# A two-layer encoder trunk with a top-2 expert FFN on one core: the row-number matmuls move to an expert's third step, the first loads change order, and the tail of the attention goes by token tile

## The chip, the cores and the metric

The kernel runs on one core of one Trainium2 chip. It is written engine by engine: TensorE (PE), VectorE (DVE), ScalarE (ACT), GpSimd (POOL) and SyncE (SP) each have a program of their own, and semaphores order them. The metric is the device time of one execution in microseconds. Before the change it is 1575.75 us, the median of 3 runs (1575.65 to 1578.21).

## The reference, cut to what matters

Two layers over 256 tokens of width 1024, all in float32.

```python
for l in range(2):
    h = rms_norm(x, g_mix[l])
    qa, ka, va, qb, kb, vb, qc, kc, vc, qd, kd, vd, fd = split(h @ w_in[l])
    oa = stick_breaking_attention(qa, ka, va)
    ob = sliding_window_sink_attention(norm(qb), norm(kb), vb, sinks, slopes)
    oc = chunked_relpos_attention(norm(qc), norm(kc), vc, rel_bias[l])
    od = forgetting_attention(norm(qd), norm(kd), vd, log_sigmoid(fd + b_f[l]))
    x = x + concat(rms_norm(o) * g_out for o in (oa, ob, oc, od)) @ w_out[l]
    h2 = rms_norm(x, g_ffn[l])
    if l == 0:   # dense, hidden width 2816
        x = x + (silu(h2 @ w_gate) * (h2 @ w_up)) @ w_down
    else:        # 8 experts of hidden width 3584, the best two for each token
        gates = softmax of the two largest of h2 @ w_router, else 0
        x = x + sum(gates[:, e] * swiglu(h2, w_gate[e], w_up[e], w_down[e]) for e in range(8))
```

## The kernel before, in words

**Tokens and weights.** The 256 tokens are two tiles of 128. SBUF holds nine units of 4096 floats per partition, through which all weights pass; only SyncE's queue loads weights. The attention's matmuls are plain float32. In the FFN each weight and each activation is split into a rounded high part and a low remainder, and a product is three matmuls: high by high, high by low, low by high (lines 825 to 827 for dense gate and up, 939 to 941 for an expert's, 849 to 851 for down). The high part is made by ScalarE (`high`, line 1139), the low part by VectorE (`low`, line 1555), each in four quarters; a quarter of a full unit is 128x1024 elements.

**Attention.** The groups come in the order D, A, C, B. `project` (line 634) multiplies by the input weights. GpSimd makes the reciprocal roots (`rstd`, lines 1240 and 1243) and, once in each layer, group C's bias table (line 1284, 8 additions). That table comes from `ext`, a scratch tensor in DRAM with each row of the relative bias extended by copies of its last element; SyncE writes it with two DMAs (`extend`, lines 488 and 491), waits for them, and loads the table with overlapping rows (`load_table`, line 496). Everything that SyncE issues behind this wait starts after it. `out_project` (line 757) sums over the groups for token tile t; the order before is D, A for tile 0, C for tile 0, D and A for tile 1, then B's transposes (line 707) and values (lines 728 to 730), C for tile 1, B for tile 0, B for tile 1. Then VectorE adds the sum to x (line 1487), ScalarE squares (line 1010), GpSimd makes the root, VectorE scales (line 1319), TensorE transposes (`norm`, line 616), and ScalarE and VectorE read the transposes (lines 1020 and 1331, in layer 1 also 1340). This is done for both tiles before the dense steps or the router (line 883) begin.

**Dense FFN.** 2816 hidden columns are a half step of 256 and five steps of 512. `hidden_cols` puts the half step first. Each step does gate and up for tile 0, down of the step before for tile 1, the transposes of the hidden product (line 834), and so on for tile 1. The hidden product needs ScalarE's SiLU (line 1152) and VectorE's product (line 1561). `steps` writes the first steps out and puts the last four into a loop of two turns.

**Experts.** At most 128 tokens go to an expert, in slots. An expert has 7 steps of 512 hidden columns. In `slots_path` a step m is: gate (`half_up(m, 0)`), up (`half_up(m, 1)`), down of the step before (`slot_down(m - 1)`), transposes of this step's product. For the next expert VectorE makes a selection matrix (`select`, line 1650) at the end of an expert's step 0; TensorE multiplies it by the token numbers (`index`, line 908) between gate and up of step 1; VectorE reads the row numbers (line 1657); GpSimd gathers the rows from DRAM (line 1297), and TensorE transposes them at the end of step 4 (line 918). GpSimd also stores each expert's output rows (line 1301).

VectorE's order in a step is: low part of the next gate, hidden product, (row numbers in step 1), low part of the next up, low part of the hidden product, low part of down, (selection in step 0). ScalarE's is: SiLU, high part of the next gate, of the next up, of the hidden product, of down.

Of the kernel before, what the change touches and what calls it, by code (L numbers as in the profile page):

```python
# [15 lines left out]
P = 128  # L16
# [4 lines left out]
L = 2  # L21
# [116 lines left out]
def trunk(nc, x_in, g_mix, w_in, b_f, g_q, g_k, swa_sinks, rel_bias, g_out, w_out, g_ffn,  # L138
          w_ff_gate, w_ff_up, w_ff_down, w_router, w_exp_gate, w_exp_up, w_exp_down, consts, out):
    with ExitStack() as ctx:  # L140
# [95 lines left out]
        oT = xs  # L236

# [45 lines left out]
        lo_ready = [sem(f"low_{kind}_ready") for kind in ("gate", "up", "down")]  # L283
        s_ext = sem("rel_bias_extended")
        s_tabc = sem("rel_table_loaded")
# [91 lines left out]
        def steps(eng, one, n, first, use, parity):  # L377
# [3 lines left out]
            peeled = n - 4  # L381
            for s in range(peeled):
                one(s, (parity + s) % 2, first + s, use + (parity + s) // 2, None)
            with eng.Fori(0, 2) as i:
# [19 lines left out]
        def unless_last(eng, s, n, loop, run):  # L404

            if s < n - 3:
                run()
                return
# [13 lines left out]
        def hidden_cols(s, dense):  # L422
            return FT // 2 if dense and s == 0 else FT
# [31 lines left out]

        block = ctx.enter_context(nc.Block())
# [3 lines left out]
        def _(sp):  # L460
# [24 lines left out]
            def extend():  # L485

                rows = ext.rearrange("l h c -> (l h) c")
                sp.dma_start(rows[:, 0:RB - 1], rel_bias.rearrange("l h c -> (l h) c")[:, 1:RB]).then_inc(s_ext, 16)
                last = bass.AP(tensor=rel_bias.tensor, offset=rel_bias.offset + RB - 1, 
                               ap=[[RB, L * H], [0, EXT - RB + 1], [1, 1]])  # L490
                sp.dma_start(rows[:, RB - 1:EXT].unsqueeze(2), last).then_inc(s_ext, 16)

            def load_table(l):

                sp.wait_ge(s_ext, 16 * 2)
                sp.dma_start(hankels[l], bass.AP(tensor=ext.tensor, offset=ext.offset + l * H * EXT,
                                             ap=[[1, P], [EXT, H], [1, T]])).then_inc(s_tabc, 16)
# [11 lines left out]
            load_w_in_d(0)  # L509
            sp.dma_start(con[:, P:C_ALL], consts[:, P:C_ALL]).then_inc(s_con, 16)  # L510
# [6 lines left out]
            load_w_in(0, "A")  # L517
            extend()
            load_table(0)
# [6 lines left out]
            def first_steps(l, gate, up, down, cols):  # L526

                if l == 0:
# [13 lines left out]
                load_up(gate, l, 1, 0, cols)  # L542
                load_up(up, l, 1, 1, cols)
                if l == 0:
                    load_down(down, l, 1, cols)
# [12 lines left out]
            with sp.Fori(1, DENSE_STEPS // 2) as i:  # L558
# [1234 lines left out]
```

## Time and profile before

| | |
|---|---|
| median of 3 runs | 1575.75 us (1575.65 to 1578.21) |
| the profiled execution | 1572.12 us, span 1570.3 us |
| mean granted TensorE clock | 0.979 of full speed |
| busy: TensorE, VectorE, ScalarE, GpSimd | 95%, 70%, 58%, 4% |
| attention 0, dense steps, attention 1 | to about 182, 376 and 545 us |
| router and experts | from 545 us to the end |

The granted clock is TensorE's: 1.00 in a stretch is 2.4 GHz, 0.50 is 1.2 GHz. In a row of the timeline the first two numbers are the start and the duration in us, then come engine, line, operation, output and inputs, shapes and the count of instructions; what stands in brackets is how long the engine had been idle before the row, and who ended that.

### The profile page before, as it was taken

The page shows a single profiled execution, that of the slowest core. Times are in us where ns is not written, and L with a number is a line of the kernel's source. Part 1 is how long each engine was busy: PE and PEld are TensorE (multiplying, and loading weights), DVE is VectorE, ACT ScalarE, POOL GpSimd, SP SyncE. Part 2 cuts the span into 40 slices and gives each one's busy share as a digit, 9 for nine tenths or more (in the row PEclk, how much of TensorE's full clock was granted, in tenths as well). Part 3 has the DMA queues.
Part 4 walks back from the last instruction along what each step waited for, and adds up shares of the span by engine and source line. Part 5 has one row for each costly group of instructions (what it writes and reads, how often), then busy time and mean ns, then how long its engine had stood idle before and what let it go on. Part 6 is the DMA issues. An engine that isn't in the chain of part 4 may idle for free.

```text
span 1570.3 us, 16689 instructions
## 1 busy us (share of the span) xinstructions
PE 1486.3 (95%) x6513; PEld 1149.1 (73%) x6513; DVE 1092.0 (70%) x1248; ACT 907.7 (58%) x1206; POOL 61.7 (4%) x99
## 2 busy tenths in 40 slices
PE   6999799998999879999999999999999999999997
PEld 3565578886565457887887887887887887888885
DVE  1244464442233467888998888898898899798894
ACT  2133343342233256777777777777777777677772
POOL 1021000000021000000000000000000000000000
PEclk9999899999999989999999999999999999999999
DMA  7710464419030248999999999999999999999992
GB/s 237 284 55 0 176 253 161 161 60 402 7 129 33 103 165 334 353 372 376 374 360 374 370 359 371 377 365 366 375 356 364 384 367 368 355 359 363 393 343 82
DMA packets 181786, 435.20 MB, mean 277 GB/s; under 512 B 6545, under 2 KB 11849, under 8 KB 181577
## 3 DMA queue, kind: packets, MB, share of 16 engines
q1 hardware_dynamic: 178824, 423.63, 73.4%
q0 software_dynamic: 2880, 10.49, 1.7%
q8 instruction: 51, 0.84, 0.2%
q14 instruction: 31, 0.25, 0.1%
HBM read 428.34 MB, written 5.78 MB: 276 GB/s over the span
## 4 chain that ended last, share of the span: by engine, by line
PE 86%; DVE 7%; ACT 2%; DMA 2%; issue 2%; SPq 1%; POOL 0%; DVEq 0%; ACTq 0%
PE ps L939 12%; PE ps L941 12%; PE ps L940 12%; PE ps L849 8%; PE ps L851 8%; PE ps L850 8%; PE ps L634 7%; PE ps L757 3%; DVE unit_rounded L1555 3%; PE ps L826 3%; PE ps L827 3%; PE ps L825 3%; DMA wmem<-in_w_in_dram 2%; PE ps L834 2%; ACT unit_rounded L1139 1%
## 5 line engine op out<-in xcount | busy, mean ns | idle before, releaser
L1555 DVE TENSOR_TENSOR unit_rounded<-wmem,unit_rounded 128x1024 fp32r<-128x1024 f32 (+1 forms) x744 | 854.4, 1211 | 90.4 <-ACT unit_rounded L1139 90.3
L1139 ACT ACTIVATE unit_rounded<-wmem 128x1024 fp32r<-128x1024 f32 (+1 forms) x744 | 719.7, 1043 | 150.2 <-PE ps L941 82.1
L849 PE MATMUL ps<-unit_rounded,vbuf_rounded 128*128 128x512 f32 x536 | 212.6, 397 | 4.5 <-DVE unit_rounded L1555 3.0
L851 PE MATMUL ps<-unit_rounded,stage_rounded 128*128 128x512 f32 x536 | 212.7, 397 | 0.0
L850 PE MATMUL ps<-unit_rounded,vbuf_rounded 128*128 128x512 f32 x536 | 212.4, 396 | 0.0
L939 PE MATMUL ps<-unit_rounded,qkT_rounded 128*128 128x512 f32 x448 | 181.4, 405 | 2.4 <-DVE qkT_rounded L1698 2.4
L940 PE MATMUL ps<-unit_rounded,qkT_rounded 128*128 128x512 f32 x448 | 178.6, 399 | 0.0
L941 PE MATMUL ps<-unit_rounded,qkT_rounded 128*128 128x512 f32 x448 | 178.5, 398 | 0.0
L939 PE MATMUL ps<-unit_rounded,hT_rounded 128*128 128x512 f32 x448 | 177.2, 396 | 0.0
L941 PE MATMUL ps<-unit_rounded,hT_rounded 128*128 128x512 f32 x448 | 174.6, 390 | 0.0
L940 PE MATMUL ps<-unit_rounded,hT_rounded 128*128 128x512 f32 x448 | 174.5, 390 | 0.0
L634 PE MATMUL ps<-wmem,hT 128*128 128x512 f32 (+2 forms) x448 | 160.7, 516 | 6.3 <-DMA wmem<-in_w_in_dram 4.9
L634 PEld LDWEIGHTS ps<-wmem,hT 128*128 128x128 f32 x448 | 85.9, 195 | 74.4 <-issue 67.3
L849 PEld LDWEIGHTS ps<-unit_rounded,vbuf_rounded 128*128 128x128 f32 x536 | 101.1, 189 | 29.1 <-issue 3.2
L851 PEld LDWEIGHTS ps<-unit_rounded,stage_rounded 128*128 128x128 f32 x536 | 101.0, 188 | 24.4
L850 PEld LDWEIGHTS ps<-unit_rounded,vbuf_rounded 128*128 128x128 f32 x536 | 101.1, 189 | 24.2
L1156 ACT ACTIVATE vbuf_rounded<-ps 128x512 fp32r<-128x512 f32 (+1 forms) x68 | 40.1, 589 | 132.4 <-PE ps L834 132.4
L939 PEld LDWEIGHTS ps<-unit_rounded,qkT_rounded 128*128 128x128 f32 x448 | 85.3, 190 | 21.8 <-DVE qkT_rounded L1698 2.6
L941 PEld LDWEIGHTS ps<-unit_rounded,qkT_rounded 128*128 128x128 f32 x448 | 85.2, 190 | 20.7
L940 PEld LDWEIGHTS ps<-unit_rounded,qkT_rounded 128*128 128x128 f32 x448 | 85.2, 190 | 19.1
L941 PEld LDWEIGHTS ps<-unit_rounded,hT_rounded 128*128 128x128 f32 x448 | 84.1, 188 | 17.8
L940 PEld LDWEIGHTS ps<-unit_rounded,hT_rounded 128*128 128x128 f32 x448 | 84.2, 188 | 16.7
(207 smaller groups left out, 1319.9 us busy)
## 6 DMA issues: line engine op xcount, KB each, us to landing
wmem<-in_w_exp_gate_dram SPq DMA_DIRECT2D x56, 2048.0 KB, 8.7
wmem<-in_w_exp_up_dram SPq DMA_DIRECT2D x56, 2048.0 KB, 9.0
wmem<-in_w_exp_down_dram SPq DMA_DIRECT2D x56, 2048.0 KB, 9.1
wmem<-in_w_in_dram SPq DMA_DIRECT2D x4, 3072.0 KB, 16.1
wmem<-in_w_ff_gate_dram SPq DMA_DIRECT2D x5, 2048.0 KB, 8.4
wmem<-in_w_ff_up_dram SPq DMA_DIRECT2D x5, 2048.0 KB, 8.6
wmem<-in_w_ff_down_dram SPq DMA_DIRECT2D x5, 2048.0 KB, 7.6
wmem<-in_w_out_dram SPq DMA_DIRECT2D x4, 2048.0 KB, 19.0
```

Of the source, the lines that this page charges most:

```text
L634: mm = pe.matmul(pbank(m)[:, 0:cols], hT[:, k, t * P:(t + 1) * P], win(l, g)[:, k, c0:c0 + cols], start=(k == 0), stop=(k == KD - 1))
L757: mm = pe.matmul(ps[:, 2 * t + half, :], oT[:, t, k * P:(k + 1) * P], wo[:, k, half * 512:(half + 1) * 512], start=(g == ORDER[0] and kk = ...
L825: pe.matmul(o, xhk, hi[:, k, :], start=(k == 0), stop=False)
L826: pe.matmul(o, xhk, lo[:, k, :], start=False, stop=False)
L849: pe.matmul(o, hhb, hi[:, b, c], start=(first and b == 0), stop=False, skip_group_check=True)
L850: pe.matmul(o, hhb, lo[:, b, c], start=False, stop=False, skip_group_check=True)
L851: mm = pe.matmul(o, hlb, hi[:, b, c], start=False, stop=(b == blocks - 1), skip_group_check=True)
L939: pe.matmul(o, xhk, hi[:, k, :], start=(k == 0), stop=False)
L940: pe.matmul(o, xhk, lo[:, k, :], start=False, stop=False)
L941: mm = pe.matmul(o, xlk, hi[:, k, :], start=False, stop=(k == KD - 1))
L1139: act.activation(quarter_r(HIGH[l][kind], q, cols), quarter(SETS[l][i][kind], q, cols), ACT.Copy).then_inc(hi_ready[kind], 1)
L1555: dve.tensor_tensor(quarter_r(u, q, cols), quarter(u, q, cols), quarter_r(HIGH[l][kind], q, cols), ALU.subtract).then_inc(lo_ready[kind], 1)
```

## The change

Three things are joined.

1. In the experts, `index` and `row_numbers` run in the step s == 2 instead of s == 1. For the very first step (m == 0) the transposes of the hidden product are issued after the gate matmuls of step 1 instead of after step 0's up matmuls.
2. The first loads: after D's weights SyncE loads the relative bias rows into SBUF (`ext_rows`, eight partitions of `osq`) and A's weights, then the constants and small tensors, C, B and w_out. GpSimd fills the tail of the rows (`extend`), writes them to `ext` in one DMA, and in layer 0 loads the table itself (`first_table`), right before it uses it. VectorE's first write of `osq` waits for the DMA out of it.
3. The attention tail goes by token tile: x of tile 0 is normed and transposed before B of tile 1 is projected; A and C of tile 1 each move back by one place. In layer 0 tile 1's transposes stand inside the first dense step, between gate and up of tile 0, and that step is ordered anew. It is a full step now; the half step is the second. The low part of the first up moves behind B's group norm. The six dense steps are written out without a loop. In layer 1 tile 1's transposes come right before the router.

```diff
-            peeled = n - 4
+            peeled = n if n == DENSE_STEPS else n - 4
...
-            return FT // 2 if dense and s == 0 else FT
+            return FT // 2 if dense and s == 1 else FT
...
             load_w_in_d(0)
+            sp.dma_start(ext_rows[:, 0:RB - 1], rel_bias.rearrange("l h c -> (l h) c")[:, 1:RB]).then_inc(s_rel, 16)
+            load_w_in(0, "A")
             sp.dma_start(con[:, P:C_ALL], consts[:, P:C_ALL]).then_inc(s_con, 16)
...
-            load_w_in(0, "A")
-            extend()
-            load_table(0)
             load_w_in(0, "C")
...
-                out_project(l, 1, ["D", "A"])
+                out_project(l, 1, ["D"])
                 p_transposes(l, "B")
                 values(l, 3, "B")
-                out_project(l, 1, ["C"])
+                out_project(l, 1, ["A"])
                 o_transposes(l, 3, "B")
                 out_project(l, 0, ["B"])
+                out_project(l, 1, ["C"])
+                norm(l, "y", (0, 1))
                 out_project(l, 1, ["B"])
-                norm(l, "y")
+                emptied(pe, l, ("y", 0))
+                emptied(pe, l, ("y", 1))
...
+                    if l == 0 and s == 0:
+                        gate_up(l, i, step, 0, src, 0, cols, 1, (0,))
+                        second_norm(l)
+                        gate_up(l, i, step, 0, src, 0, cols, 1, (1,))
+                        second_ready(l)
+                        gate_up(l, i, step, 1, src, 1, cols, 1, (0,))
+                        transposes(0, cols, step * 2 + 1, 1)
+                        gate_up(l, i, step, 1, src, 1, cols, 1, (1,))
+                        down(l, i, step, 0, 0, cols, step * 2 + 1, 1, first=True)
+                        transposes(1, cols, step * 2 + 2, 1)
+                        return
...
                     half_up(m, 0)
-                    if e + 1 < E and s == 1:
+                    if e + 1 < E and s == 2:
                         index(e + 1)
+                    if m == 1:
+                        transposes(0, FT, DENSE_STEPS * 2 + 2, 2)
                     half_up(m, 1)
                     if m:
                         slot_down(m - 1)
-                    transposes(m % 2, FT, (DENSE_STEPS + m) * 2 + 2, 2)
+                        transposes(m % 2, FT, (DENSE_STEPS + m) * 2 + 2, 2)
...
+            def extend():
+                pool.wait_ge(s_rel, 16)
+                pool.tensor_copy(ext_rows[:, RB - 1:EXT], ext_rows[:, RB - 2:RB - 1].broadcast_to([L * H, EXT - RB + 1])) \
+                    .then_inc(s_tail, 1)
+                pool.wait_ge(s_tail, 1)
+                pool.dma_start(ext.rearrange("l h c -> (l h) c"), ext_rows).then_inc(s_ext, 16)
+
+            def first_table():
+                pool.wait_ge(s_ext, 16)
+                pool.dma_start(hankels[0], table_rows(0)).then_inc(s_tabc[0], 16)
...
-                for kind in range(2 - l):
-                    low(l, 0, kind, l * DENSE_STEPS, hidden_cols(0, l == 0))
+                low(l, 0, 0, l * DENSE_STEPS)
                 read_p(l, "B")
                 inverse(l, "B")
                 group_out(l, 3, "B")
+                if l == 0:
+                    low(0, 0, 1, 0)
                 for t in range(NT):
                     add_out(l, t)
                     norm_scale(l, "y", t)
-                norm_read(l, "y")
+                    norm_read(l, "y", (t,))
...
-                    if e + 1 < E and s == 1:
+                    if e + 1 < E and s == 2:
                         row_numbers(e + 1)
```

## Rows read from the trace of the kernel before

**Rows 1.** The page: busy time of each engine, and the chain by engine.
```profile
PE 1486.3 (95%) x6513; PEld 1149.1 (73%) x6513; DVE 1092.0 (70%) x1248; ACT 907.7 (58%) x1206; POOL 61.7 (4%) x99
...
PE 86%; DVE 7%; ACT 2%; DMA 2%; issue 2%; SPq 1%; POOL 0%; DVEq 0%; ACTq 0%
```

**Rows 2.** Waits of TensorE, 560 us to the end: total, times, longest.
```profile
PE ps L908 <- DVE osq L1650: 10.0, 6, 3.8
...
PE ps L834 <- DVE sq L1561: 2.6, 1, 2.6
...
PE ps L908 <- DVE osq L1652: 1.7, 1, 1.7
```

**Rows 3.** Timeline of TensorE: first projection of A, and of C.
```profile
40.33 9.36 PE L634 MATMUL ps<-wmem,hT 128*128 128x512 f32 x16 [4.88 <-DMA wmem<-in_w_in_dram]
...
75.18 7.08 PE L634 MATMUL ps<-wmem,hT 128*128 128x512 f32 x16
```

**Rows 4.** Timeline of SyncE's queue: A's load, the table's load.
```profile
11.06 0.67 SPq L462 DMA_DIRECT2D wmem<-in_w_in_dram  x1
...
47.50 0.38 SPq L496 DMA_DIRECT2D wmem<-ext_rel_bias  x1
```

**Rows 5.** Stretches of 2 us: busy by engine, PEclk, DMA share, GB/s.
```profile
8.00:10.00 2.00, 1.21 (x6) 1.22 (x7) 1.45 (x3) 0.00 (x0) 0.00 (x0) 1.00 1.06 408
...
34.00:36.00 2.00, 1.45 (x7) 0.92 (x5) 0.00 (x0) 0.45 (x2) 0.00 (x0) 1.00 0.81 29
```

**Rows 6.** Timeline of GpSimd: the table's additions and C's root.
```profile
77.98 4.01 POOL L1284 TENSOR_TENSOR wmem<-wmem,con 128x128 f32<-128x128 f32 x8
88.29 0.20 POOL L1240 TENSOR_SCALAR rq<-ssq 128x8 f32<-128x8 f32 x1 [6.30 <-DVE ssq L1360]
```

**Rows 7.** Timeline of VectorE: the first operation behind C's first unit.
```profile
93.44 1.76 DVE L1539 TENSOR_TENSOR wmem<-wmem 128x1536 f32<-128x1536 f32 x1 [2.43 <-ACT wmem L1074]
```

**Rows 8.** GpSimd's stores of 512 KB (line 1301).
```profile
DMA to landing us min/median/max: 8.5/8.8/9.5
```

**Rows 9.** SyncE's two loads of the table (line 496).
```profile
DMA to landing us min/median/max: 5.2/9.1/13.1
```

**Rows 10.** Timeline of TensorE: tail of attention 0, first dense step.
```profile
156.70 0.41 PE L728 MATMUL ps<-vbuf,wmem 128*128 128x64 f32 x2 [0.63 <-ACT wmem L1083]
...
164.57 7.13 PE L757 MATMUL ps<-wmem,xs 128*128 128x512 f32 x16 [0.93 <-ACT xs L1090]
...
177.22 2.06 PE L616 MATMUL ps<-con,xs 128*128 128x128 f32 x8 [4.12 <-DVE hT_rounded L1331]
181.78 0.55 PE L825 MATMUL ps<-unit_rounded,qkT_rounded 128*128 128x256 f32 x1 [2.50 <-issue]
...
189.63 0.44 PE L834 MATMUL ps<-con,sq 128*128 128x128 f32 x2 [0.59 <-DVE sq L1561]
```

**Rows 11.** Timeline of VectorE in the same stretch.
```profile
154.58 0.56 DVE L1444 COPY wmem<-ps 128x384 f32<-128x384 f32 x1 [2.00 <-PE ps L707]
...
175.29 0.75 DVE L1319 TENSOR_SCALAR xs<-x,rx 128x1024 f32<-128x1024 f32 x1 [2.14 <-POOL rx L1243]
```

**Rows 12.** Timeline of TensorE: tail of attention 1, router.
```profile
542.36 1.13 PE L616 MATMUL ps<-con,xs 128*128 128x128 f32 x8 [3.68 <-DVE hT L1340]
544.76 6.96 PE L883 MATMUL ps<-wr,hT 128*128 128x8 f32 x32 [1.28 <-issue]
```

**Rows 13.** Timeline of TensorE: step 1 of expert 0.
```profile
591.99 1.01 PE L908 MATMUL ps<-con,osq 128*128 128x1 f32 x4 [3.81 <-DVE osq L1650]
...
600.80 0.40 PE L849 MATMUL ps<-unit_rounded,vbuf_rounded 128*128 128x512 f32 x1
...
606.41 0.60 PE L834 MATMUL ps<-con,obuf 128*128 128x128 f32 x4
```

**Rows 14.** Timeline of VectorE: hidden product in step 1 of expert 1.
```profile
724.14 0.69 DVE L1561 TENSOR_TENSOR sq<-ps,sq 128x512 f32<-128x512 f32 x1 [1.31 <-PE ps L941]
```

**Rows 15.** A stretch of 40 us in the experts, columns as in rows 5.
```profile
1480.00:1520.00 40.00, 40.00 (x182) 32.83 (x181) 36.70 (x36) 29.32 (x34) 3.15 (x2) 1.00 1.04 394
```

More of the change, by code:

```diff
@@ L404, in unless_last @@
         def unless_last(eng, s, n, loop, run):
+            if loop is None:
+                if s < n - 1:
+                    run()
+                return
             if s < n - 3:
@@ L524, in _, with first_steps @@
             sp.dma_start(wr[:], w_router[0].rearrange("(k p) e -> p k e", p=P)).then_inc(s_wr, 16)
-            def first_steps(l, gate, up, down, cols):
+            def first_steps(l, gate, up, down, second):
+                cols = FT
                 if l == 0:
@@ L557, in _ @@
             first_steps(0, *dense, FT // 2)
-            with sp.Fori(1, DENSE_STEPS // 2) as i:
-                f0 = i * (2 * FT) - FT // 2
-                step(0, 0, (0, 1, 2), dense, f0, sp.snap(i * 2))
-                step(0, 1, (0, 1, 2), dense, f0 + FT, sp.snap(i * 2 + 1))
+            for s in range(2, DENSE_STEPS):
+                step(0, s % 2, (0, 1, 2), dense, s * FT - FT // 2, s)
             for done in (g_full, u_full, d_full):
@@ L605, in open_fill, with norm @@
                     pe.wait_ge(tr_free[n % 2], l * (NFILL // 2) + n // 2)
-            def norm(l, name):
-                for i in range(4):
+            def norm(l, name, parts=range(4)):
+                for i in parts:
                     t = i // 2
@@ L998, in norm, with read @@
                 y = name == "y"
+                parts = y and l == 0
+                def read(i):
+                    t = i // 2
+                    filled(act, l, (name, i))
+                    for b in range(4):
+                        k = 4 * (i % 2) + b
+                        c = (G_FFN if y else G_MIX) + l * KD + k
+                        ins = act.activation((xh_r if parts else hT)[:, k, t * P:(t + 1) * P],
+                                             bank((name, i))[:, b * P:(b + 1) * P], ACT.Copy, scale=gT[:, c:c + 1])
+                    ins.then_inc(xh_ready if parts else tr_free[1], 1)
                 for t in range(NT):
@@ L1469, in group_out @@
                 emptied(dve, l, (g, "o"))
+                if l == 0 and gi == 0:
+                    dve.wait_ge(s_ext, 16)
                 for t in range(NT):
```

76 lines of the change are left out of this document (42 added, 34 removed).

## The prediction

> **What bounds the kernel now.** The page first: TensorE is busy 95% of the span and holds 86% of the chain that ended last [rows 1]. So only what TensorE waits for, and the time that it runs on the lower clock, can be won; VectorE at 70% matters where it is the one waited for. The list of waits of the experts' stage says who that is: seven waits on line 908, 11.7 us together and 3.8 at most, and one of 2.6 us on line 834 [rows 2]. The timeline of TensorE at the start, at the end of each attention and at the first expert gives the rest. The reader is to see a gap ahead of a row, and after a long gap longer matmuls.
>
> **The sum, part by part.** Positions are those of the profiled execution (1572.12 us, span 1570.3); the median of the runs is 3.6 us above it.
>
> (a) *Order of the first loads.* The first projection of A waited 4.88 us for its weights and then took 9.36 us for 16 matmuls; 16 like it take 7.08 at full clock [rows 3]. TensorE had been free at 35.45. The load was issued at 11.06, behind 1.9 MB of constants and three small loads, and landed after 29.1 us. The reason is in the windows: full rate at 8 us (408 GB/s), and at 34 us a busy share of 0.81 with 29 GB/s [rows 5], which is the 1,024 four-byte elements of the old table tail. These are gone, and A goes out before the constants, near 7 us. Behind D's 3 MB its own 3.1 MB need 7.7 us at 408 GB/s: it lands at 20 to 24, over 10 us before its use. Gain 4.88 + 9.36 - 7.08 = 7.2 us. The constants and the small loads come 8 us later, near 32; their first readers on the path are the forget sums, now at 42. I take 7.2, bounds 4 (a late small load eats 3) and 8. C, B and w_out no longer stand behind a queue that waits until 47.50 for the extended table [rows 4]; nothing waited for them, so that is worth nothing here.
>
> (b) *Table through GpSimd's queue.* GpSimd now issues the 512 KB table load itself after line 1243's work and waits for it before its 4.01 us of additions; the next thing behind it on GpSimd is C's reciprocal root, whose input comes at 88.2 [rows 6]. VectorE waits for that result (line 1378, 0.7 us) before line 1539, which ScalarE releases at 93.44 [rows 7]. So 78.0 + L + 4.05 + 1.95 + 0.8 must stay under 93.4: a landing L up to 8.6 us is free, each us beyond is paid. On this queue 512 KB landed in 8.5 to 9.5 us under the weight stream [rows 8]; this table itself, from SyncE's queue, in 5.2 and 13.1 [rows 9], the 5.2 on empty engines, as they are here. I take nothing; bounds 0 and 4.5 (13.1).
> The Trainium skill ("SBUF — State Buffer", section "SBUF: two separate sides") says that a DMA issued by GpSimd can't get its descriptors written while VectorE holds the shared port in some copies; no run here shows it so far. Its page "DMA: Bandwidth & Descriptors" (section "Anatomy of one DMA — SWDGE (gpsimd) path") gives 2.0 us and the bytes at 436 GB/s, some 3.2 us for this load as an estimate; the trace's 8.5 us is far longer.
>
> (c) *Tail of attention 0 and the dense steps.* Only D of tile 1 stands before the B transposes, so TensorE is there 3.5 us sooner (8 of 16 matmuls in 7.13 [rows 10]). Their third head needs VectorE, free at 152.6 before [rows 11] and at 152.3 now (one full conversion, 4.6 us, for two half ones). It copies at 152.3 instead of 154.58: 2.3 us won, the other 1.2 a new wait. The values start at 154.4 instead of 156.70, A hides the group's norm as C did, and B of tile 0 ends at 165.8. The second conversion, now behind the group's norm, ends at 165.2, just as the sum needs VectorE. C of tile 1 to 169.4; scaled x of tile 0 comes at 169.7; 8 transposes (1.1); B of tile 1 ends at 174.3 (171.7 before). The first dense gate starts at 174.4 and lasts 5.6 us (24 matmuls, as between the last two of [rows 13]). Before, it started at 181.78 after gaps of 4.12 and 2.50, and its 48 half matmuls took 7.26 us on a clock that had fallen, for 5.65 at full clock [rows 10]. Tile 1's scaled x is ready 4.35 after B's end (176.04 against 171.70 [rows 10, 11]), so at 178.7, under the gate matmuls that end at 180.0. Gain: 7.4 of start, less 1.05 for tile 1's transposes still to come, 1.5 of clock, two waits of 0.6 for the hidden values [rows 10] now covered by tile 1's gate, less 0.5 for a new one in the half step (ScalarE makes a full gate's high part and the SiLU within it) = 8.5. The half step itself moves no work. Bounds 5 (VectorE or ScalarE late once more in each new place) and 10. The dense steps as straight code: no gap stands at the old loop's turns, so nothing.
>
> (d) *Tail of attention 1.* The same order, but nothing after it covers tile 1. B of tile 1 ends 2.6 us later than before (as in c: 174.3 for 171.7), then 4.3 to the scaled x, 1.1 of transposes, 1.2 for ScalarE's read: the router starts 6.7 after B's end, where it took 7.5 (544.76, with B's end at 537.3: 542.36 less the gap of 3.68, 1.1 of transposes and 0.3 before them [rows 12]). Loss 2.6 - 0.8 = 1.8 us. Bounds 1 and 3.5 (transposes also on the low clock).
>
> (e) *First expert.* The transposes of step 0 move behind the gate matmuls of step 1. The conversions allow it: the product now waited for stands behind all four quarters of step 1's gate on VectorE, so they are there by 581.3, and matmuls from 579.3 on need the last of them at 583.5. The 2.6 us wait goes. Line 908 moves to the third step; there the selection is long done. The 3.8 us go, with 24 matmuls that took 7.8 us (593.0 to 600.80) where 24 take 5.6, and 0.4 of the index matmuls themselves [rows 13]. What is late next is step 1's hidden product: VectorE ends it at 597.2 (selection's end at 591.99, a conversion of 4.6, a product of 0.6), TensorE would be there at 596.5 (579.3, three times 5.6, transposes 0.4): with their hand-over 0.9 back. 2.6 + 3.8 + 2.2 + 0.4 - 0.9 = 8.1. Bounds 5 and 9.
>
> (f) *The six other experts.* 11.7 - 3.8 = 7.9 us [rows 2]. Behind them nothing stands close: at the boundary VectorE waited 1.31 us itself for TensorE [rows 14], and the product it makes there is due only after the 5.6 us down projection. VectorE no longer waits in the second step but reads the row numbers in the third, where it does nothing else new. 7.9, bounds 4 and 8.
>
> Sum: 7.2 + 0 + 8.5 - 1.8 + 8.1 + 7.9 = 29.9 us. The profiled 1572.1 becomes 1542.2, and the median of 1575.75 becomes 1546.
>
> **Rivals.** *1. The weight stream becomes the bound.* In the experts' stage the DMA engines have a share near 1.0. If they can't deliver faster than now, (e) and (f) come back as waits for weights: 29.9 - 16.0 = 13.9 us, 1562. Against it: a stretch of 40 us ran at 394 GB/s [rows 15], while a step of 17.2 us (72 matmuls at 5.61 for 24, and the transposes, [rows 13]) needs 6.29 MB, 366 GB/s; and a load has a whole step to land. 0.10.
> The Trainium skill ("DMA: Bandwidth & Descriptors", section "Where 436 GB/s comes from") has the memory bind at about 358 GB/s for a core. By that rule rival 1 would hold in full; the row above already passes its figure.
> *2. The front part gives little.* GpSimd's table lands at 13, the small loads come late, the reordered tail meets VectorE in each new place: (a) 4, (b) -4.5, (c) 5, (d) -3.5: 17.0 in all, 1559. For it: many margins are under 1 us. Against it: they would have to fail together; one or two alone give 1549 to 1554. 0.15.
> *3. Slower: the gathered rows come late.* The index is now one step later, and the row transposes of the fifth step need it, GpSimd's gather and its landing. From the new place to the fifth step's end are 2 x 17.2 + 11.4 = 45.8 us; VectorE's read within 17 and a landing of 9.5 (the same queue's store [rows 8]) leave 19. It decides only if the gather takes 28 us or more; seven times 4.3 us beyond that cancel all gain, and any more is slower, say 1580. 0.02 slower, 0.01 near nothing.
> *4. The change doesn't do what it says:* the waits on line 908 reappear in the third step since VectorE is late by a conversion there too. That keeps (a) to (d) and loses (f) and most of (e): 1560, or no change with rival 2 on top. 0.04, of which 0.01 no change.
>
> **The numbers.** Forecast 1546, chance 0.68; its own range is 1541 to 1552. Rivals as above. The range that holds 8 in 10 reaches from 1540 (upper bounds in c and e) to 1557, which takes in the weaker half of rival 2. This kernel's runs can't tell a change under 0.2% (3 us) from none. Faster 0.96, same 0.02, slower 0.02.
>
> **What would show it.** Right: A's first projection starts near 35.5 with no gap; line 908 has no wait; the first dense gate starts about 14 us earlier than 181.8 (7.2 of a, 7.4 of c) at full clock; the router starts 1.8 us later relative to its attention; step 2 of the first expert starts 30 us after its step 0 instead of 39. Wrong: waits of TensorE for VectorE's line 1555 or for ScalarE in the experts, a line 1539 released by line 1378, a low clock stretch in a new place, or a step period above 17.2 us in the experts.

## The result, and the profile after

The changed kernel takes 1538.13 us in the median of 4 runs (1537.91 to 1541.07); the kernel before took 1576.98 in the same comparison (4 runs, 1575.65 to 1580.45). The ratio is 0.9753, interval 0.9731 to 0.9776. Forecast were 1546 and a range from 1540: the sign and the places were right, the gain was 8 us larger, and the time lies 2 us below the range.

The profiled execution took 1537.91 us, its span is 1536.1. The page of the changed kernel, busy time, granted clock by slices, and the chain by engine; they answer to [rows 1].

```profile
span 1536.1 us, 16565 instructions
PE 1474.5 (96%) x6513; PEld 1143.5 (74%) x6513; DVE 1090.8 (71%) x1248; ACT 907.7 (59%) x1206; POOL 68.9 (4%) x102
...
PEclk9999999999999889999999999999999999999999
...
PE 90%; DVE 6%; ACT 2%; issue 1%; POOL 0%; SPq 0%; DMA 0%; DVEq 0%; ACTq 0%
```

TensorE has the same 6513 matmuls and is busy 11.8 us less: matmuls that ran on the low clock now run on the high one. The other 22 us are idle time that is gone.

The waits of TensorE from 560 us to the end of the changed kernel; they answer to [rows 2]. The two lines that had waited 14.3 us no longer do: no wait stands on the index matmuls (now line 934), and the transposes (line 847) wait 0.7.

```profile
PE ps L862 <- DVE unit_rounded L1609: 3.0, 1, 3.0
PE ps L978 <- DVE x L1767: 0.9, 1, 0.9
PE ps L978 <- DVE con L1761: 0.8, 1, 0.8
PE ps L847 <- DVE obuf L1615: 0.7, 1, 0.7
```

The timeline of TensorE of the changed kernel, from first projections to first scores: start, duration, then the group. D's last units and A's first run on without a gap, in one row of 32 records, where [rows 3] had 4.88 us of waiting and a slow projection. In their place a stretch of low clock has appeared behind the 2.02 us wait of line 687: the second four matmuls of that line take 0.80 for 0.65, and the next projection starts at 50.26.

```profile
31.26 10.64 PE L636 MATMUL ps<-wmem,hT 128*128 128x260 f32 x32 [0.72 <-DVE stage L1429]
...
47.41 0.65 PE L687 MATMUL ps<-qkT 64*128 64x128 f32 x4 [2.02 <-DVE qkT L460]
47.83 1.08 PE L688 MATMUL ps<-qkT 64*128 64x256 f32 x4
48.68 0.80 PE L687 MATMUL ps<-qkT 64*128 64x128 f32 x4
...
50.26 7.94 PE L636 MATMUL ps<-wmem,hT 128*128 128x512 f32 x18
```

GpSimd of the changed kernel around the table, as [rows 6]; the load is issued at 71.78, and its own view adds "DMA to landing us min/median/max: 4.1/4.1/4.1".

```profile
71.78 0.89 POOL L1311 DMA_DIRECT2D wmem<-ext_rel_bias  x1
75.92 3.89 POOL L1335 TENSOR_TENSOR wmem<-wmem,con 128x128 f32<-128x128 f32 x8 [3.25 <-DMA wmem<-ext_rel_bias]
82.11 0.20 POOL L1276 TENSOR_SCALAR rq<-ssq 128x8 f32<-128x8 f32 x1 [2.30 <-DVE ssq L1411]
```

The tail of attention 0 and the first dense gate, TensorE; they answer to [rows 10].

```profile
148.13 0.41 PE L730 MATMUL ps<-vbuf,wmem 128*128 128x64 f32 x2 [0.63 <-ACT wmem L1118]
...
156.01 7.13 PE L759 MATMUL ps<-wmem,xs 128*128 128x512 f32 x16 [0.93 <-ACT xs L1125]
163.44 1.09 PE L618 MATMUL ps<-con,xs 128*128 128x128 f32 x8 [0.30 <-DVE xs L1370]
164.37 3.60 PE L759 MATMUL ps<-wmem,xs 128*128 128x512 f32 x8
167.57 0.63 PE L838 MATMUL ps<-unit_rounded,qkT_rounded 128*128 128x512 f32 x1
```

From the first values to the first gate it took 25.1 us before; now it takes 19.4, at full clock and without a wait above 0.93. The tail of attention 1 and the router, as [rows 12]: the wait grew from 3.68 to 4.47, and the transposes fell to the low clock (1.94 for 1.13).

```profile
526.98 1.94 PE L618 MATMUL ps<-con,xs 128*128 128x128 f32 x8 [4.47 <-DVE xs L1370]
530.20 6.97 PE L909 MATMUL ps<-wr,hT 128*128 128x8 f32 x32 [1.28 <-issue]
```

The first expert, as [rows 13]: transposes early, index matmuls in the third step with no wait ahead of them.

```profile
582.75 0.66 PE L847 MATMUL ps<-con,obuf 128*128 128x128 f32 x4 [0.70 <-DVE obuf L1615]
...
588.85 0.50 PE L934 MATMUL ps<-con,osq 128*128 128x1 f32 x4
589.21 0.48 PE L965 MATMUL ps<-unit_rounded,qkT_rounded 128*128 128x512 f32 x1
```

Where the 34.2 us between the two profiled spans went, by the places where both timelines pass the same instruction: first loads 6.2, the new low stretch already taken off; tail of attention 0 and dense steps 9.3; less low clock in attention 1, 1.7; tail of attention 1 up to the router -2.65, and 0.1 more up to the first expert; first expert 8.7; six other experts 11.1.

The 1.7 us are luck of the two executions and not the change. The kernel before had 375 to 390 us and 465 to 480 us at a granted clock of 0.77 each, the changed one 360 to 375 us at 0.89 and 400 to 410 us at 0.83. A second execution of the kernel before, below, has 370 to 380 us at 0.83, 410 to 416 us at 0.72 and no low clock from 455 to 480 us, much as the changed kernel.

### The profile page after: what moved, and what is told of

It is laid out like the page before. It is cut to its first block, busy times and chain, and to the rows that moved or that the text cites. A ratio compares the mean times of both kernels' runs of the same rounds, so it can differ in the third digit from the quotient of the medians.

```text
span 1536.1 us, 16565 instructions
## 1 busy us (share of the span) xinstructions
PE 1474.5 (96%) x6513; PEld 1143.5 (74%) x6513; DVE 1090.8 (71%) x1248; ACT 907.7 (59%) x1206; POOL 68.9 (4%) x102
## 4 chain that ended last, share of the span: by engine, by line
PE 90%; DVE 6%; ACT 2%; issue 1%; POOL 0%; SPq 0%; DMA 0%; DVEq 0%; ACTq 0%
PE ps L965 13%; PE ps L967 13%; PE ps L966 13%; PE ps L862 8%; PE ps L864 8%; PE ps L863 8%; PE ps L636 8%; PE ps L839 3%; PE ps L840 3%; PE ps L838 3%; PE ps L759 2%; DVE unit_rounded L1609 2%; PE ps L847 2%; PE ps L618 1%; PE ps L730 1%
## 5 line engine op out<-in xcount | busy, mean ns | idle before, releaser
L965 PEld LDWEIGHTS ps<-unit_rounded,qkT_rounded 128*128 128x128 f32 x448 | 84.2, 188 | 21.6 <-DVE qkT_rounded L1753 2.6
L967 PEld LDWEIGHTS ps<-unit_rounded,qkT_rounded 128*128 128x128 f32 x448 | 84.1, 188 | 20.4
L966 PEld LDWEIGHTS ps<-unit_rounded,qkT_rounded 128*128 128x128 f32 x448 | 84.2, 188 | 18.9
L967 PEld LDWEIGHTS ps<-unit_rounded,hT_rounded 128*128 128x128 f32 x448 | 84.1, 188 | 17.8
```

The costliest lines, as they stand in the source:

```text
L965: pe.matmul(o, xhk, hi[:, k, :], start=(k == 0), stop=False)
L966: pe.matmul(o, xhk, lo[:, k, :], start=False, stop=False)
L967: mm = pe.matmul(o, xlk, hi[:, k, :], start=False, stop=(k == KD - 1))
```

## The experiments

**One part alone.** Each of these is the kernel before with one part of the change. *The index and the row numbers in the third step:*

```
-                    if e + 1 < E and s == 1:
+                    if e + 1 < E and s == 2:      (index and row_numbers)
```


> The kernel before with one edit: index and row_numbers run in step 2 instead of step 1. Theory 1 (a wait on line 908 costs more than its idle time: the restart behind it, and in some of them a stretch on the low clock): from the profiled executions each of the six later boundaries is worth 1.6 us instead of 1.3, the last one 1.5 more for its low clock, the first one 3.8 + 2.2 + 0.4: about 17 to 18 us off the span of 1570.3, so near 1553, and 20 us or more between the medians, since other executions of the kernel before hit the low clock more often. Theory 2 (only the listed idle time is won, as the prediction counted): 11.7 + 2.6 = 14.3 us, no more in the medians. Theory 3 (the wait comes back elsewhere): under 5 us.

Measured: 1556.98 us (1555.02 to 1561.25), ratio 0.9871 [0.983, 0.9912]; span 1555.8. The waits on the row numbers are all gone. The span fell by 14.5 us only, which looks like theory 2, and the medians differ by 19.4. But what stands ahead of the experts had come out 3.6 us slower in this execution, as the table below shows. From the first expert's first matmul to the last row transposes it takes 810.8 us where the kernel before takes 828.6: 17.8 us, as theory 1 has it.

*The transposes of step 0 early, the index left where it was:*

```
                     half_up(m, 0)
+                    if m == 1:
+                        transposes(0, FT, DENSE_STEPS * 2 + 2, 2)
                     if e + 1 < E and s == 1: index(e + 1)
...
                     if m:
                         slot_down(m - 1)
-                    transposes(m % 2, FT, (DENSE_STEPS + m) * 2 + 2, 2)
+                        transposes(m % 2, FT, (DENSE_STEPS + m) * 2 + 2, 2)
```


> The kernel before with one edit: in the first expert the transposes of step 0's hidden product stand behind the gate matmuls of step 1, ahead of the row-number matmuls, which stay in step 1. Theory 1: nothing is won. The 2.6 us wait on line 834 goes, but VectorE's chain, not TensorE, sets when the selection is made (592.0), so the wait on line 908 grows by the same 2.6 us to 6 or 7; within 1 us of before, perhaps 1 us slower by a longer low clock. Rival: the 2.6 us are won, span near 1567.7.

Measured: 1575.89 us, ratio 0.9989 [0.9965, 1.0014], nothing. The waits of TensorE in the experts say why, beside [rows 2]: line 834's 2.6 us are gone, and the longest on line 908 is 6.8 instead of 3.8. VectorE ends its chain when it did, and TensorE only waits at the next place.

```profile
PE ps L908 <- DVE osq L1652: 12.9, 6, 6.8
```

*Both edits of the experts together:*


> The kernel before with the index and the row numbers in an expert's third step and the transposes of step 0 early (both edits of the experts, nothing of loads or tail). Theory 1: the two edits together bring all that the changed kernel won from the first expert on, 8.3 us there and 11.4 us in the six others: span 1572.1 - 19.7 = 1552.4 us, 2.6 to 4 us under the kernel with the index alone (span 1555.8). Rival: part of the 19.7 us came from the other edits (weights loaded earlier, a shifted clock); then the span stays at 1554 us or more.

Measured: 1554.95 us, ratio 0.9872 [0.9847, 0.9897]; span 1553.3. From the first expert's first matmul to the last row transposes it takes 808.8 us, the same in the changed kernel, 828.6 in the kernel before: the two edits are all of it. The early transposes, worth nothing alone, bring 2.0 us on top of the index alone (810.8). The expectation took the 19.7 us off the execution's 1572.1 us and not off its span of 1570.3; set right it is 1550.6, and the span is 2.7 above that: the first expert began 1.3 us later than in the first execution, and the last 25 us had more low clock (0.50 from 1535 to 1540), 1.4 us.

*The first loads alone* (A's weights ahead of the constants, the table extended on GpSimd and loaded by its queue):

```
+            sp.dma_start(ext_rows[:, 0:RB - 1], rel_bias...[:, 1:RB]).then_inc(s_rel, 16)
+            load_w_in(0, "A")
...
-            load_w_in(0, "A")
-            extend()
-            load_table(0)
```


> The kernel before with the second part of the change alone: order of the first loads, table rows extended by GpSimd, table of layer 0 loaded by GpSimd. Theory 1: 4.9 us of waiting and 2.5 us of low clock go, but a new stretch on the low clock follows the 2.0 us gap before the first scores, 1.6 us: 6.2 us off the span, near 1564. Rival (the new low clock belongs to the joined kernel, not to this part): 7.5 to 8 us, near 1562.5.

Measured: 1565.13 us (8 runs, 1563.4 to 1566.31), ratio 0.9925 [0.99, 0.995]; span 1564.5, as forecast. But the medians differ by 11.3 us and not by 6 or 7, and these 8 runs lie within 3 us, where the kernel before had 24 from 1572.02 to 1586.71.

*The tail by token tile and the dense steps alone:*

```
-                out_project(l, 1, ["D", "A"])
+                out_project(l, 1, ["D"])
...
+                norm(l, "y", (0, 1))
+                out_project(l, 1, ["B"])
```


> The kernel before with the third part alone: attention tail by token tile, first dense step reordered, half step second, dense steps without a loop. Theory 1: 9.3 us won in layer 0, 2.7 us lost in layer 1: 6.6 us off the span, near 1563.7, give or take 2 us for where the low clock falls in attention 1. Rival (the tail and the dense step are worth little without the earlier start): under 4 us.

Measured: 1571.38 us (1563.94 to 1576.93), ratio 0.9954 [0.9928, 0.998]; span 1570.7, not 1563.7. From the first values to the first dense gate it took 19.45 us, just as in the changed kernel, so the tail does what it should. The rest was lost at 35 us, long before: the wait for A's weights, 4.88 in [rows 3], was 10.87 here.

```profile
46.23 9.93 PE L639 MATMUL ps<-wmem,hT 128*128 128x512 f32 x16 [10.87 <-DMA wmem<-in_w_in_dram]
```

**The kernel before once more,** to see what an ordinary execution of it is:


> The kernel before, unchanged, profiled once more. Its first profiled execution took 1572.1 us where its median was 1575.75, so that its rows may be those of a lucky execution. Theory 1: an ordinary execution has all the work and waits of the first one (waits on the row numbers 10.0 us in all), and is longer only by stretches of low clock behind waits of 1 to 2 us: if this execution takes 1575 us or more, its windows show at least one more low-clock stretch than the first one's, or a longer one, and the rest agrees within 1 us. Rival: the longer ones have longer waits for DMA or for the other engines at full clock.

Measured: 1573.99 us (1564.08 to 1582.08), the profiled one the shortest of all, 1564.08. So it does not show what an execution of 1575 us or more looks like, but it can be held against the first one, whose span is 8.1 us longer. Both theories have a part. The waits of TensorE agree line by line within 0.4 us but for one: it waits 0.6 us for A's weights. The projection behind it runs at full clock. At the end of that projection the two executions are already 7.5 us apart.

```profile
35.13 7.11 PE L634 MATMUL ps<-wmem,hT 128*128 128x512 f32 x16 [0.60 <-DMA wmem<-in_w_in_dram]
```

Up to 30 us the DMA engines moved about the same in both executions. Behind it they moved 277 and 39 GB/s here in the stretches from 30 and from 32 us, 194 and 22 GB/s in the first one, which went on at 29 and 19.

With all profiled executions side by side (us; T0 is the first expert's first matmul):

```
kernel                      wait for A's weights   T0      T0 to end
before                      4.9                    567.8   1002.5
before again                0.6                    559.7   1002.5
index alone                 7.5                    571.4    984.4
transposes alone            8.3                    569.4   1002.7
tail alone                 10.9                    567.9   1002.8
before, waits filled        9.7                    571.3    998.6
index and transposes        4.6                    569.1    984.2
loads alone                 0                      561.8   1002.7
changed                     0                      553.4    982.7
changed again               0                      551.5    983.0
```

The experts' stage repeats within 0.3 us wherever its code is the same, but for the 1.4 us of low clock at the end of the kernel with index and transposes. The rest of what moves between these executions lies ahead of T0. With the old loads the wait for A's weights was anything from 0.6 to 10.9 us, 6.6 in the mean of seven; with the new loads there was none in any of the seven profiled executions that have them (the three here and the four kernels below). Which part of the edit does that no run separates: it takes the 1,024 four-byte elements away and moves A ahead of the constants and the small loads at once.

**What a short wait costs in clock.** *The kernel before with its waits at the index filled* by dummy matmuls, whose results nobody reads; nothing else, and the waits' ends don't move:

```
+                for _ in range(14 if e == 1 else 5):
+                    pe.matmul(ps[:, 5, :], xeh_r[(e - 1) % 2][:, 0, :], <four blocks of the same>, ...)
                 pe.wait_ge(sel_ready, e + 1)          (index)
```


> The kernel before, with dummy matmuls (gathered rows by themselves, 128 x 512, 0.23 us each: 5 at a boundary, 14 at the first) in TensorE's waits ahead of the row-number matmuls; the waits' ends do not move. Theory 1: the waits of 1.3 us themselves stay, and only the stretches of low clock that follow them in some executions go: span near 1570.6 us (1.5 less than 1572.1), the median falls from 1576.5 to within 2 us of the span, and the runs lie within 4 us of each other instead of 14. Rival: the scatter has another source: median near 1576.5 us with runs still 10 us and more apart.

Measured: 1571.62 us (1559.14 to 1576.02), ratio 0.9968 [0.9947, 0.9989]; span 1569.9. The scatter stayed, 17 us, so theory 1 is wrong there; the loads alone had left 3 us of it. (The runs of the changed kernel's second measurement, below, are 8 us apart, so the first load is not all of it.) But T0 to end fell from 1002.5 to 998.6, though all work and all waits' ends stand where they did. The windows at the first and the last boundary show it; in the kernel before again, the last boundary looks as in the second view (1319.69 is the last matmul ahead of the wait).

```profile
590.00:595.00 5.00, 4.84 (x22) 3.61 (x20) 5.00 (x6) 4.26 (x6) 0.00 (x0) 1.00 1.02 403
1330.00:1335.00 5.00, 4.49 (x22) 3.44 (x21) 4.93 (x9) 3.83 (x5) 0.00 (x0) 1.00 1.03 408
```

```profile
1319.69 0.40 PE L941 MATMUL ps<-unit_rounded,qkT_rounded 128*128 128x512 f32 x1
1321.75 0.61 PE L908 MATMUL ps<-con,osq 128*128 128x1 f32 x4 [1.66 <-DVE osq L1652]
1322.22 0.48 PE L939 MATMUL ps<-unit_rounded,qkT_rounded 128*128 128x512 f32 x1
...
1323.39 0.63 PE L940 MATMUL ps<-unit_rounded,qkT_rounded 128*128 128x512 f32 x1
1323.82 0.63 PE L941 MATMUL ps<-unit_rounded,qkT_rounded 128*128 128x512 f32 x1
...
1326.65 0.39 PE L939 MATMUL ps<-unit_rounded,qkT_rounded 128*128 128x512 f32 x1
```

A wait of 1.66 us is followed by eight matmuls that start 0.43 us apart instead of 0.233: 1.6 us on top; of the six boundaries behind the first expert only the last one has it. And each boundary costs more than its listed wait: from the matmul ahead of the wait to the one behind the index 2.53 us pass here (1319.69 to 1322.22); in the changed kernel 0.60 (1314.62 to 1315.22, first view below). That is 1.93 for a wait listed with 1.66. The second view below has the next two boundaries behind the first in the kernel before, with waits of 1.28 and 1.15: from start to start 2.13 us at the former (716.14 to 718.27), 1.53 more than 0.60.

```profile
1314.62 0.40 PE L967 MATMUL ps<-unit_rounded,qkT_rounded 128*128 128x512 f32 x1
1314.86 0.50 PE L934 MATMUL ps<-con,osq 128*128 128x1 f32 x4
1315.22 0.48 PE L965 MATMUL ps<-unit_rounded,qkT_rounded 128*128 128x512 f32 x1
```

```profile
716.14 0.39 PE L941 MATMUL ps<-unit_rounded,hT_rounded 128*128 128x512 f32 x1
717.81 0.61 PE L908 MATMUL ps<-con,osq 128*128 128x1 f32 x4 [1.28 <-DVE osq L1650]
718.27 0.48 PE L939 MATMUL ps<-unit_rounded,hT_rounded 128*128 128x512 f32 x1
...
839.68 0.61 PE L908 MATMUL ps<-con,osq 128*128 128x1 f32 x4 [1.15 <-DVE osq L1650]
```

*The changed kernel with a part of the next projection drawn into the wait ahead of the first scores:*

```
-                scores(l, 0, "D")
-                project(l, "A", 1)
+                project(l, "A", 1, range(2))
+                scores(l, 0, "D")
+                project(l, "A", 1, range(2, KD))
```


> The changed kernel, with the first 2 of the 8 k-blocks of the projection A unit 1 placed ahead of the first scores in both layers (they came behind), so that the wait of 2.02 us for the scaled q and k is filled with real work. Theory 1: the wait goes (2.02 to 0.3) and with it the low-clock stretch behind it (about 1.6 us), 3.3 us in each layer: span near 1529.5 us, median near 1531.5 us. Rival: the softmax of group D ends no earlier and the 4.1 us of waits ahead of the transposes of p take up what is won: at least 1537 us.

Measured: 1540.69 us (1533.13 to 1543.44), ratio 0.978 [0.9754, 0.9806]; span 1531.3. The profiled execution did what theory 1 said at that place (wait 0.30, full clock) and was 4.8 us shorter; the other runs were not, at granted clocks of 0.980 to 0.984 where it had 0.988. It shows already how that comes about. A wait of 1.25 us further on, which the changed kernel has too, at 99.33, with no low clock behind it there, here is followed by one: the eight transposes of line 650 take 2.16 us, in the changed kernel 0.61 and 0.66 for four each.

```profile
95.32 0.43 PE L733 MATMUL ps<-vbuf,wmem 128*128 128x64 f32 x2 [1.25 <-ACT wmem L1117]
...
98.36 2.16 PE L650 MATMUL ps<-con,stage 128*128 128x128 f32 x8
101.50 0.81 PE L690 MATMUL ps<-qkT 64*128 64x128 f32 x4 [0.97 <-DVE qkT L460]
```

So in these executions the clock's fall after a short wait is no property of that wait alone. Nor does this run show that filling the wait is what kept the clock up at the first scores: the second execution of the changed kernel, below, has the wait of 2.02 us and full clock there. Why the slower runs were slower no profile here shows.

**The end of attention 1.** *The changed kernel with layer 1's tail in its old order:*

```
-                out_project(l, 1, ["D"])
+                out_project(l, 1, ["D"] if l == 0 else ["D", "A"])
...
+                if l:
+                    out_project(l, 1, ["B"])
+                    norm(l, "y")
```


> The changed kernel, with the attention tail of layer 1 alone put back into its old order (out-projection of token tile 1 early, norm of both tiles behind it). Theory 1: ordering the tail by token tile costs 2.65 us in layer 1, because no work follows tile 0 there before the router; span 1536.1 - 2.65 = 1533.4 us, about 1535.5 us in the median, ratio near 0.974. Rival: the 2.65 us is not the order but where the stretches of low clock happened to fall; then the time stays at 1538 us (within 1 us).

Measured: 1535.50 us (1533.87 to 1538.96), ratio 0.9752 [0.9725, 0.9778]; span 1532.0. The median is 2.6 us under the result's, as theory 1 has it, but the two come from different comparisons and their ratios are the same (0.9752 and 0.9753), so the medians alone don't decide. The traces do: from the start of the out-projections ahead of B's transposes to the first expert it takes 61.4 us in the changed kernel (492.00 to 553.35) and 58.6 here (490.46 to 549.04), as in the kernel before. The other 1.5 us by which this span is shorter lie ahead of it. The last wait is 3.69 again, and the one for VectorE's copy of the third head is 0.3 where it is 1.4 in the changed kernel, as the prediction had it for layer 0.

*The changed kernel with 27 dummy matmuls between the last norm and the first expert:*

```
+            keep(9, 5)        (9 dummies, 128 x 256, into bank 5, ahead of the last transposes)
+            keep(2, 3)        (ahead of the router, behind its wait)
+            keep(6, 3)        (behind the router)
+            keep(5, 3)        (behind the mask matmuls), keep(5, 3) (behind the gather)
```


> The changed kernel, with 27 dummy matmuls (con by con, 128 x 256, nobody reads them) in TensorE's waits of 1.3 to 4.5 us from the last norm to the first expert; nothing else changed. Theory 1: TensorE's idle waits bring the clock to its low level there (0.50 at 530 to 545 us), and kept busy it stays high: the norm's transposes 1.94 to 1.1, the router 6.97 to 3.5, the mask matmuls 2.3 to 1.2, the gather 5.88 to 2.95, in all 8.3 us; span near 1528 us, median near 1530 us. Rival: the clock falls there for another reason, or the dummy matmuls delay what follows: 1538 to 1541 us and a granted clock still at 0.50 from 530 to 545 us.

Measured: 1536.03 us (1534.68 to 1541.24), ratio 0.9752 [0.9724, 0.9779], that of the result within its interval; span 1537.3, 1.2 longer than the changed kernel's. The transposes kept full clock (1.09), but a wait of 1.33 us was left ahead of the router's dummies, which start at 530.02. From there the clock is low although TensorE was busy all the time, and it comes back only behind the 12 wider matmuls (dummies of 256 columns) that follow the router; the columns are PE, PEld, DVE, ACT, POOL, then PEclk.

```profile
530.00:535.00 5.00, 4.98 (x21) 4.65 (x21) 0.00 (x0) 0.00 (x0) 0.00 (x0) 0.52 0.98 356
535.00:540.00 5.00, 5.00 (x21) 4.73 (x22) 1.21 (x7) 0.00 (x0) 0.00 (x0) 0.50 0.80 311
540.00:545.00 5.00, 5.00 (x20) 4.19 (x20) 2.39 (x14) 0.20 (x1) 0.00 (x0) 0.62 0.00 0
```

*The same on top of the old tail, the dummies of the router's wait moved ahead of it, and one of 128 columns behind every second router matmul:*

```
                    mm = pe.matmul(ps[:, 0, t * E:(t + 1) * E], hT[...], wr[:, k, :], ...)
+                    if k % 2:
+                        keep(1, 3, 128)
```


> The changed kernel with the old tail in layer 1 (as in e5) and dummy matmuls in TensorE's waits from the last norm to the first expert, this time also ahead of the wait for hT, and one of 128 columns behind every second of the router's 16 matmuls of 8 columns: in e6 the clock stayed at 0.50 through the router although TensorE was busy at 4.98 of 5 us. Theory 1: matmuls of 8 columns do not hold the clock and the dummies between them do; from e5's span of 1532.0: router 6.96 to 5.3 with its dummies in, mask matmuls 2.3 to 1.2, gather 5.82 to 2.95, together 5.6 us: span near 1526.4 us, median near 1528 to 1530 us. Rival: the clock stays low there whatever TensorE does; the dummies then cost 2 to 4 us, span 1534 to 1536 us.

Measured: 1532.35 us (1529.48 to 1534.09), ratio 0.9722 [0.9695, 0.975]; span 1531.5, clock 0.993. The router with its eight dummies takes 5.4 us (6.97 alone) and starts at full clock.

```profile
525.00:530.00 5.00, 4.32 (x34) 3.93 (x34) 0.81 (x2) 1.14 (x4) 0.36 (x1) 1.00 1.04 355
530.00:535.00 5.00, 5.00 (x32) 4.73 (x32) 1.61 (x10) 0.00 (x0) 0.00 (x0) 0.76 1.03 406
...
540.00:545.00 5.00, 4.80 (x38) 4.41 (x37) 4.52 (x6) 5.00 (x10) 0.00 (x0) 1.00 0.01 3
```

Half of the 5.6 us came: from the end of the last out-projection to the first expert 27.5 us instead of 30.5 in the kernel with the old tail. In the span only 0.5 is left of these 3.0 (1531.5 for 1532.0): in this execution the last out-projection ended 1.7 us later and the experts took 0.8 longer. A low stretch was left behind the router, dummies there delayed the mask matmuls by 0.7, and the gather, now 3.84 us, is followed by 3.3 us until the first gate where there were 2.4: the evictions on VectorE and ScalarE end last there.

*The changed kernel itself, beside it:*


> The changed kernel itself, so that e9 and e5 have it in the same comparison: 1538 us in the median (within 1 us), span 1536, the same short stretches of low clock at 45 to 55 and 400 to 410 us if the profiled execution is of the same kind. If its median lies above 1539.5 us, the 1538.13 us of the result was luck of the clock.

Measured: 1538.85 us (1536.35 to 1544.68), ratio 0.9781 [0.9752, 0.9809]. It stayed under the 1539.5 us that would have called the result luck. The kernel with the old tail in layer 1 and the dummies beats it by 6.5 us in the same comparison: the two intervals only just do not meet. This execution's first scores stand behind the same wait of 2.02 us as in the first view of the changed kernel, and no low clock follows them:

```profile
46.24 0.50 PE L687 MATMUL ps<-qkT 64*128 64x128 f32 x4 [2.02 <-DVE qkT L460]
46.57 0.61 PE L688 MATMUL ps<-qkT 64*128 64x256 f32 x4
47.00 0.49 PE L687 MATMUL ps<-qkT 64*128 64x128 f32 x4
...
47.86 4.56 PE L636 MATMUL ps<-wmem,hT 128*128 128x512 f32 x10
```

## Why the prediction was right in kind and wrong in size

The forecast missed by 7.9 us: 4.3 in the sum (34.2 for 29.9) and 3.6 in the step from the profiled execution to the median.

(f) *is the term of the sum that failed:* 11.1 for 7.9, above its upper bound of 8. The prediction took the waits as the list gives them: three of 1.28, two of 1.15, the last of 1.66. From row transposes to row transposes of the next expert the change gave 1.58, 1.43, 1.60, 1.43, 1.56 and 3.48 us, together 11.1. That is some 0.3 more than the listed wait each time, and 1.6 of low clock besides at the last. The first I could have read in the timeline, from start to start; the second too, since in [rows 13] I had counted just such a stretch, 2.2 us, for the first boundary, and did not look behind the others. The filled waits show the clock's part, 3.9 us of both boundaries together. The upper bound of 8 allowed for no more than the listed waits.

What put the time under 1540 is neither miss alone. With (f) at 11.1 the forecast would have been 1542.6 us; with the offset right and (f) as it was, 1542.4. Nor could the bounds reach what was measured: all upper bounds together make 34.0 us, a median near 1542, so the range's edge at 1540 was not their sum either.

(e) 8.7 for 8.1, right (the expectations have 8.3 and 11.4 for (e) and (f); counted at the row transposes it is 8.7 and 11.1). The transposes alone won nothing and the pair did, as its steps say: one chain on VectorE stood behind both waits. The new wait behind it is 0.70 (0.9 forecast).

(c) 9.3 for 8.5. The gate started 14.2 us earlier (167.57 for 181.78), where 14.6 were expected (that less a of 6.2 is 8.0 for the tail, 7.4 forecast). The new waits in the half step that I charged with 0.5 did not come.

(d) -2.65 for -1.8, and the mechanism is shown by the old tail, whose trace gives it all back. My credit of 0.8 at the transposes wasn't there, for they ran on the low clock, which I had named as a bound only.

(a) 6.2 for 7.2 in the profiled pair: A's load was issued at 9.33 us and landed after 13.8, at 23.1, where 20 to 24 were forecast; the gap went, and at least 1.2 us came back as the low stretch behind the first scores (2.85 us from 47.41 to 50.26; 1.62 in the second execution of the changed kernel, which has none). In the medians, though, the loads alone bring 11.3. The rows showed one draw of a wait that lies anywhere between 0.6 and 10.9. I priced it as if it were fixed. The reason given for it is not tested either. The load went late while the engines moved 20 to 30 GB/s, as [rows 5] say; but they had also moved only 37 and 105 GB/s from 20 to 24 us, ahead of A's bytes, which the prediction does not mention, and no run takes the four-byte elements away alone.

(b) 0, right: landing 4.1, where 8.6 would have been free. The Trainium skill ("DMA: Bandwidth & Descriptors", section "Anatomy of one DMA — SWDGE (gpsimd) path") gave some 3.2 us as an estimate; the trace has 4.1, with a DMA share of 0.27 from 70 to 76 us, nearer to it than to the 8.5 us that the stores took under the weight stream [rows 8]. Whether VectorE's copies hold such a DMA back was not seen: 3.25 us of waiting behind the issue is all there is.

*From the profiled execution to the median.* I carried the 3.6 us by which the kernel before was above its profiled execution over to the changed one, where the profiled run and the median differ by 0.2. That offset was no constant but scatter, of either sign: in the seven profiled executions with the new loads the kernel's median lies from 3.0 us below to 7.6 us above the profiled one, in the second measurement of the kernel before 9.9 above. The first load's wait and the low clock behind it, which the change removes, are a part of it (4.9 us in the profiled execution, 6.6 in the mean of seven); what the rest is no profile shows. That the changed kernel's own offset was near nothing was luck, and in the later comparison (1574.29 against 1538.85) the difference is 35.4 us, so the result's 38.9 has some scatter of its own. The 1.7 us of clock in attention 1, in no term of the sum, were luck as well.

*The rivals.* 1, the weight stream: false. The experts' DMA share is 1.04 and no wait for a weight appears; a stretch of 40 us, as [rows 15], moves 393 GB/s. The Trainium skill ("DMA: Bandwidth & Descriptors", section "Where 436 GB/s comes from") has the memory bind at about 358 for a core; the measured rate is above it, and it decides.

```profile
1440.00:1480.00 40.00, 40.00 (x180) 32.80 (x179) 36.98 (x36) 30.27 (x34) 3.16 (x2) 1.00 1.04 393
```

2: false in every part but (d), whose -2.65 lies midway between the forecast and this rival's -3.5. 3 and 4: the index stands in the third step without a wait, and the row transposes behind it wait for nothing.

## What to carry to other kernels

A wait in a list can be less than it costs, as at all seven places here: measure it from the start of the instruction before it to the start of the one behind, and look behind it for matmuls at the long spacing. Both went here when the wait went, but a stretch of low clock can turn up behind another short wait. Before costing a wait for a DMA from one execution, ask what stands in the queue around it; where that can vary, take a second execution. The offset from the profiled run to the median is scatter of one execution: it belongs into the range and not into the forecast. When two waits stand on one chain of another engine, removing the first alone moves it to the second.

## What was not expected of the hardware

Matmuls of 8 columns, back to back, did not bring the clock back: TensorE was busy 4.98 and 5.00 of 5 us at 0.52 and 0.50. With one dummy of 128 columns behind every second one the same stretch began at 1.00; but there the wait of 1.33 us ahead of the router was down to 0.41 as well, and which of the two did it no run shows. The same wait of 2.02 us, in two executions of one kernel, was once followed by a low clock and once not. And the load of 3 MB for A took 24.0 us from issue to landing in one execution of the kernel before, 29.1 in another and 35.0 with the tail changed alone, with the same DMAs ahead of it and the same 1,024 reads of four bytes issued behind it.
